# FFN input projection with the weights stationary and 256 tokens streamed, its product made feature-major and its transposes left out

## The reference

```python
D_MODEL, SEQ, D_FF = 2048, 256, 5632

def rmsnorm(x, g):
    y = x * lax.rsqrt(jnp.mean(x * x, axis=-1, keepdims=True) + EPS)
    return y * g

def swiglu(h, w_in, w_out):          # w_in 2048 x 11264, w_out 5632 x 2048
    gu = h @ w_in
    gate, up = gu[..., :D_FF], gu[..., D_FF:]
    return (jax.nn.silu(gate) * up) @ w_out

h = h + 0.5 * swiglu(rmsnorm(h, ffn1_norm[l]), ffn1_w_in[l], ffn1_w_out[l])
...
h = h + 0.5 * swiglu(rmsnorm(h, ffn2_norm[l]), ffn2_w_in[l], ffn2_w_out[l])
```

## Time and profile before

| | us |
|---|---|
| median of 3 runs | 2803.59 |
| the runs | 2803.33, 2803.59, 2807.78 |
| profiled execution: its own time | 2807.78 |
| profiled execution: span, first to last instruction | 2805.2 |
| TensorE (matmul) busy in the span | 2759.7 |
| weight loads busy | 2265.7 |
| VectorE busy | 1489.3 |
| ScalarE busy | 1272.2 |
| DMA | 506 MB, 180 GB/s |

### The profile page before, as it was taken

The page is one execution under the profiler, slowest core; times in us unless marked ns, Lnnn a source line. Parts: engine busy times, 40 slices in busy tenths (PEclk is TensorE's granted clock), DMA queues, the critical chain, the costliest instruction groups (busy, mean ns, idle before and its releaser), DMA issues.

```text
span 2805.2 us, 34347 instructions
## 1 busy us (share of the span) xinstructions
PE 2759.7 (98%) x12534; PEld 2265.7 (81%) x12534; DVE 1489.3 (53%) x1689; ACT 1272.2 (45%) x1621; POOL 57.1 (2%) x68
## 2 busy tenths in 40 slices
PE   8999999999999999999999999999999999999999
PEld 6888888888878788888888888877888778778877
DVE  5445455554634455555455455557655665555564
ACT  5443444344544445443444344544544444554443
POOL 0000000000000000000000000020000000120000
PEclk9999999999999999999999999999999999999999
DMA  8666666665645456655665665644456556546654
GB/s 276 189 188 194 189 190 190 193 190 162 205 137 165 149 193 187 191 188 192 190 188 191 192 193 162 201 158 150 150 186 187 159 185 188 156 139 195 181 154 139
DMA packets 375319, 506.04 MB, mean 180 GB/s; under 512 B 35831, under 2 KB 228545, under 8 KB 374417
## 3 DMA queue, kind: packets, MB, share of 16 engines
q1 hardware_dynamic: 373376, 495.84, 56.9%
q0 software_dynamic: 1632, 8.34, 0.8%
q10 hardware_dynamic: 176, 0.07, 0.0%
HBM read 502.03 MB, written 2.10 MB: 180 GB/s over the span
## 4 chain that ended last, share of the span: by engine, by line
PE 95%; DVE 2%; ACT 1%; POOL 1%; DMA 1%; issue 0%; SPq 0%; ACTq 0%; DVEq 0%
PE bank L1268 30%; PE bank L1270 29%; PE bank L1269 29%; PE bank L1226 2%; DVE wlo L1494 1%; ACT whi L1332 1%; DMA h<-in_x_dram 1%; POOL rope_b L849 1%; PE bank L996 0%; PE bank L797 0%; PE bank L781 0%; PE bank L1013 0%; PE bank L1022 0%; PE bank L488 0%; DVE iwork L922 0%
## 5 line engine op out<-in xcount | busy, mean ns | idle before, releaser
L1494 DVE TENSOR_TENSOR wlo<-raw,whi 128x1024 fp32r<-128x1024 f32 (+2 forms) x976 | 1154.7, 1187 | 1248.9 <-ACT whi L1332 1244.8
L1332 ACT CAST whi<-raw 128x1024 fp32r<-128x1024 f32 (+2 forms) x976 | 988.4, 1016 | 1374.9 <-PE bank L1270 1369.9
L1268 PE MATMUL bank<-whi,p_hi 128*128 128x512 f32 x2016 | 799.4, 397 | 5.9 <-DVE wlo L1494 5.8
L1270 PE MATMUL bank<-whi,p_lo 128*128 128x512 f32 x2016 | 787.1, 390 | 0.0
L1269 PE MATMUL bank<-wlo,p_hi 128*128 128x512 f32 x2016 | 786.6, 390 | 0.0
L1268 PE MATMUL bank<-whi,q_hi 128*128 128x512 f32 x1696 | 668.9, 394 | 5.3 <-DVE wlo L1494 5.2
L1270 PE MATMUL bank<-whi,q_lo 128*128 128x512 f32 x1696 | 661.5, 390 | 0.0
L1269 PE MATMUL bank<-wlo,q_hi 128*128 128x512 f32 x1696 | 661.2, 390 | 0.0
L1268 PEld LDWEIGHTS bank<-whi,p_hi 128*128 128x128 f32 x2016 | 379.9, 188 | 91.7 <-issue 15.3
L1269 PEld LDWEIGHTS bank<-wlo,p_hi 128*128 128x128 f32 x2016 | 380.1, 189 | 79.9 <-issue 3.1
L1270 PEld LDWEIGHTS bank<-whi,p_lo 128*128 128x128 f32 x2016 | 379.5, 188 | 80.5
(11 more groups left out here) (253 smaller groups left out, 954.7 us busy)
## 6 DMA issues: line engine op xcount, KB each, us to landing
raw<-in_ffn_w_in_dram SPq DMA_DIRECT2D x704, 256.0 KB, 2.9
raw<-in_ffn_w_out_dram SPq DMA_DIRECT2D x320, 256.0 KB, 3.0
raw<-in_w_in_a_dram SPq DMA_DIRECT2D x192, 256.0 KB, 3.0
raw<-in_w_in_mix_dram SPq DMA_DIRECT2D x128, 256.0 KB, 3.1
raw<-in_w_ple_gate_dram SPq DMA_DIRECT2D x128, 256.0 KB, 3.5
raw<-in_w_in_b_dram SPq DMA_DIRECT2D x128, 256.0 KB, 3.1
raw<-in_w_out_mix_dram SPq DMA_DIRECT2D x64, 256.0 KB, 3.2
raw<-in_w_o_a_dram SPq DMA_DIRECT2D x64, 256.0 KB, 3.4
```

The lines of the kernel that those rows point to most:

```text
L1268: pe.matmul(o, xht, wh, start=(kt == t_first), stop=False)
L1270: ins = pe.matmul(o, xlt, wh, start=False, stop=(kt == t_last))
L1332: act.copy(whi[:, c % SPLIT, 0:n, 0:w], raw[:, c, 0:n, 0:w]).then_inc(hi_done, 1)
L1494: dve.tensor_tensor(wlo[:, c % SPLIT, 0:n, 0:w], raw[:, c, 0:n, 0:w], whi[:, c % SPLIT, 0:n, 0:w].bitcast(F32), ALU.subtract).then_inc(lo_ ...
```

## The change

- In `ffn_in` stages `multiply` makes the weights stationary (128 features by 128 columns, four such blocks `m` of a tile's 512) and streams the 256 tokens. The gate sums of a round land in the first bank of its pair, the up sums in the second, both feature-major: 128 columns of the FFN on the partitions, tokens along the free axis.
- `rstd` is then needed along the free axis. `rstd_row` copies it into a 128x128 block for each half of the tokens (`rspread`), TensorE transposes the two blocks (L1105 of the changed kernel, behind chunk 1 of round 1 of `ffn1_in0` and `ffn2_in0`), VectorE copies the result to `rrow`, 256 tokens wide and the same on each partition.
- `evacuate` of `ffn_in` is now: VectorE multiplies the gate bank by `rrow` into `sg` and the up bank by `rrow` into `hid`, ScalarE applies silu to `sg` in SBUF, VectorE multiplies `hid` by `sg`. VectorE so waits for ScalarE in the middle.
- The transposes of `hid` are gone with their semaphore counts; ScalarE and VectorE split `hid` straight from SBUF (`hidden_hi`, `hidden_lo`) at the place where they split the bank before. `ffn_out` waits on `hid_done` in its first round.

The diff, cut to its core:

```diff
@@ -163,8 +163,9 @@
         h = sb("h", [P, TT, D])
-        at = overlaid([("tm", [P, TT, D], F32)], [("hid", [P, 2, TT, HB], F32)])
-        tm, hid = at["tm"], at["hid"]
+        at = overlaid([("tm", [P, TT, D], F32)],
+                      [("hid", [P, 2, 2, SEQ], F32), ("rspread", [P, TT, P], F32), ("rrow", [P, SEQ], F32)])
+        tm, hid, rspread, rrow = at["tm"], at["hid"], at["rspread"], at["rrow"]
         ab = overlaid([("bc", [P, 2, D], F32)],
@@ -287,10 +287,12 @@
-        n, latest = 0, {}
+        n, hids, latest = 0, 0, {}
         for s in stages:
                 b.number, latest[b.pair, b.kt], n = n, n, n + 1
+            if s.kind == "ffn_in":
+                s.hid0, hids = hids, hids + s.n
             for k in range(s.n):
@@ -1097,6 +1097,13 @@
                 filled(pe.transpose(use("gains")[:, 0:GAINS], vrow[0:GAINS, :], ident[0:GAINS, 0:GAINS]), "gains")
+            if stage in ROW_OF and (k, c) == (1, 1):
+                name = ROW_OF[stage]
+                pe.wait_ge(sem("rstd_spread"), int(name[-1]) + 1)
+                b = use(name)
+                for t in range(TT):
+                    ins = pe.transpose(b[:, t * P:(t + 1) * P], rspread[:, t, :], ident)
+                filled(ins, name)
             gla_pe(pe, stage, k, c)
@@ -1117,6 +1124,8 @@
             attention_b_dve(dve, link, stage, k, c)
+
+        ROW_OF = dict(ffn1_in0="rrow0", ffn2_in0="rrow1")
@@ -1203,26 +1212,16 @@
             def transposes(s, b, u):
-                number, parity, pair, kt, gain = resolve(s, b, u)
+                number, parity, pair, kt, gain = b.number, b.number % 2, b.pair, b.kt, b.gain
                 dst = bank[4 + parity]
-                if isinstance(b, Batch):
-                    issued[0] = number + 1
-                if not isinstance(b, Batch) or number >= 2:
+                issued[0] = number + 1
+                if number >= 2:
                     pe.wait_ge(freed_s[4 + parity], emitted[4 + parity])
-                if isinstance(b, tuple):
-
-                    pe.wait_ge(acc_free, s.a0 + b[1] + FREE0)
-                    src = [hid[:, (u - 1) % 2, t, j * P:(j + 1) * P] for j in range(2) for t in range(TT)]
-                elif isinstance(b.source, tuple):
-                    pe.wait_ge(acc_free, s.a0 + FREE0)
-                    src = [hid[:, b.source[0], t, j * P:(j + 1) * P] for j in range(2) for t in range(TT)]
-                else:
-                    src = b.source(kt)
-                for n, piece in enumerate(src):
+                for n, piece in enumerate(b.source(kt)):
                     ins = pe.transpose(dst[:, n * P:(n + 1) * P], piece, ident)
@@ -1252,6 +1251,16 @@
                 for j, kt in enumerate(tiles):
+                    if s.kind == "ffn_in":
+
+                        wh, wl = whi[:, c % SPLIT, j, :], wlo[:, c % SPLIT, j, :]
+                        for m in range(4):
+                            o = dst[m // 2][:, m % 2 * SEQ:(m % 2 + 1) * SEQ]
+                            f = slice(m * P, (m + 1) * P)
+                            pe.matmul(o, wh[:, f], xh[:, kt, :], start=(kt == t_first and m % 2 == 0), stop=False, skip_group_check=True)
+                            pe.matmul(o, wl[:, f], xh[:, kt, :], start=False, stop=False, skip_group_check=True)
+                            ins = pe.matmul(o, wh[:, f], xl[:, kt, :], start=False, stop=(kt == t_last), skip_group_check=True)
+                        continue
                     for t in range(TT):
@@ -1308,7 +1317,10 @@
                                 pe.wait_ge(sem("pool_split"), c + 1)
-                            pe.wait_ge(t_done, s.need[c])
+                            if s.kind == "ffn_out":
+                                pe.wait_ge(hid_done, s.hid_of.hid0 + s.chunk_tiles(c)[-1] // 2 + 1)
+                            else:
+                                pe.wait_ge(t_done, s.need[c])
                         ins = multiply(s, k, u, c, dst, tiles[0], 1 if s.kind == "ple" else tiles[-1])
@@ -1344,6 +1356,11 @@
+            def hidden_hi(s, k, u):
+
+                act.wait_ge(hid_ready, s.hid0 + k + 1)
+                act.copy(pair_hi[s.hid_pair][:, bass.ds(k * 2, 2), :], hid[:, u, :, :]).then_inc(hid_hi, 1)
+
             squared = [0]
@@ -1368,10 +1385,8 @@
                 if s.kind == "ffn_in":
-                    sums_done(act, s, k)
-                    for t in range(TT):
-                        ins = act.activation(sg[:, u, t, :], pair[t][:, 0:HB], ACT.Silu, scale=rstd[:, t:t + 1])
-                    ins.then_inc(silu_done, 1)
+                    act.wait_ge(scaled, s.hid0 + k + 1)
+                    act.activation(sgw[:, u, :], sgw[:, u, :], ACT.Silu).then_inc(silu_done, 1)
                 elif s.name in ("ffn1_out2", "mix_out", "ffn2_out2"):
@@ -1454,6 +1469,9 @@
                         operand_hi(s, b, u)
+                    made = hidden_of(s, k, u, peeled)
+                    if made:
+                        hidden_hi(*made)
@@ -1508,6 +1526,22 @@
+            def hidden_lo(s, k, u):
+
+                dve.wait_ge(hid_hi, s.hid0 + k + 1)
+                at_ = bass.ds(k * 2, 2)
+                dve.tensor_tensor(pair_lo[s.hid_pair][:, at_, :], hid[:, u, :, :], pair_hi[s.hid_pair][:, at_, :].bitcast(F32),
+                                  ALU.subtract).then_inc(hid_done, 1)
+
+            def rstd_row(name):
+
+                for t in range(TT):
+                    ins = dve.tensor_copy(rspread[:, t, :], rstd[:, t:t + 1].to_broadcast([P, P]))
+                ins.then_inc(sem("rstd_spread"), 1)
+                b = take(dve, name)
+                release(dve.tensor_copy(rrow[:, :], b[:, 0:SEQ]), name)
+                wait_freed(dve, name)
+
             def rms(n):
@@ -1521,11 +1555,13 @@
+                    sums_done(dve, s, k)
+                    row = rrow[:, :].unsqueeze(1).to_broadcast([P, 2, SEQ])
+                    dve.tensor_tensor(sg[:, u, :, :], pair[0][:, :].rearrange("p (j n) -> p j n", j=2), row, ALU.mult).then_inc(scaled, 1)
+                    dve.tensor_tensor(hid[:, u, :, :], pair[1][:, :].rearrange("p (j n) -> p j n", j=2), row, ALU.mult).then_inc(acc_free, 1)
+                    dve.wait_ge(acc_free, at_ + FREE0)
                     dve.wait_ge(silu_done, silu_before(s) + k + 1)
-                    for t in range(TT):
-                        ins = dve.scalar_tensor_tensor(hid[:, u, t, :], pair[t][:, HB:NB], rstd[:, t:t + 1],
-                                                       sg[:, u, t, :], ALU.mult, ALU.mult)
-                    ins.then_inc(acc_free, 1)
+                    dve.tensor_tensor(hid[:, u, :, :], hid[:, u, :, :], sg[:, u, :, :], ALU.mult).then_inc(hid_ready, 1)
                 elif s.kind in ("ffn_out", "mix_out", "ln_out"):
@@ -1629,12 +1665,17 @@
                         operand_lo(s, b, u)
+                    made = hidden_of(s, k, u, peeled)
+                    if made:
+                        hidden_lo(*made)
                     if not (peeled and k == s.n - 1):
                         rms(NORMED.index(s.name))
+                        if s.name in ROW_OF:
+                            rstd_row(ROW_OF[s.name])
                     evacuate(s, k, u)
                         angles(dve, link)
```

31 lines of the change are left out of this document (14 added, 17 removed).

## The result

| | us |
|---|---|
| median of the changed kernel (4 runs) | 2842.15 |
| its runs | 2840.90 to 2843.06 |
| median of the kernel before beside it (4 runs) | 2804.93 |
| ratio, 95% interval | 1.0128 [1.0116, 1.0140] |
| span of the profiled execution after | 2840.9 |

The changed kernel is 37.2 us slower. I had forecast 18.1 us faster and a range up to 2815: the sign was missed, and the time lies outside the range.

The account below looks back on a forecast made before the run. TensorE's rate of starting matmuls was taken as the bound. Transposes -20.2, split 0, row transposes +0.4 and stalls +1.7 gave -18.1 us, from 2803.6 to 2785.5 us; range 2781 to 2815, the forecast's own 2781 to 2791.

Parts of the forecast that it names:

- The step of 256 columns: ffn_in on TensorE: 4224 matmuls of 512 columns become 8448 of 256, step 0.1134 us, cost 0.
- Rival 2: TensorE matmuls: each instruction has a fixed part of 0.0031 us, +13.1 us, 2798.6 us in all; chance 0.12.
- Rival 1: ffn_in matmuls: successive loads hold back starts, step 0.1167 us, +27.9, 2813.4 us; chance 0.23, including steps up to 0.118.
- Rival 3: ffn_in weight loads not hidden behind 256 columns: +630 us, 3415 us; chance 0.04, shared with a far undersized wait.
- Transposes gone: TensorE in ffn_in: 176 transposes of hid removed, four in each of 44 rounds at 0.46 us a round, -20.2 us.
- row transposes: TensorE: two transposes of rspread in each of two stages, 4 x 0.11 us, +0.4 us.
- hand-over in `ffn1_in0`: After round 0 the evacuation chain starts late, so TensorE stalls before chunk 4 of round 1: +1.6 us, once.
- in `ffn2_in0`: The same late chain, without angles, before chunk 4: +0.1 us.
- Cost 0 in steady rounds and at `ffn1_out2`: Added ScalarE and VectorE work stays covered: 4.7 us slack in steady rounds, 0.5 us before chunk 6 of ffn1_out2.
- The signs that I named: Profile checks: step 0.113 us, two ffn_in rounds 43.5 us, one ffn1_in0 gap of 1 to 2 us; wrong above 0.1155.

Follow-up runs that it names:

- e1_half_stream: The kernel before, with each ffn_in matmul of 512 streamed columns issued as two of 256 on the same stationary block; 2859.04 us, ratio 1.0185.
- e7_long_streams: e4_old_product with stationary width and streamed length (288 to 512) set per ffn_in stage, inner tiles only, sums incomplete; 2643.37 us in one run.
- e3_stream_by_stage: The changed kernel with 248 down to 64 tokens streamed per ffn_in stage behind 128 stationary columns, sums incomplete; 2895.42 us in one run.
- e4_old_product: The changed kernel with the token-major product of 512 columns put back in ffn_in, output not the reference's; 2789.50 us, ratio 0.9937.

## Why the prediction failed

- **The step of 256 columns: this is what failed.** I wrote "By this row the split costs 0" and took 0.1134, half of 0.2268, with "no fixed part for an instruction". The step is 0.1200. That is above both ends of what I had bounded (0.1134 and 0.1167), and in place of 0 stands +55.8 us. Two errors lie in it. The one: I read the equality of the earlier trace rows with half of the earlier trace rows as proportionality. The earlier trace rows alone spoke against it: 512 columns at 2.4 GHz are 0.2133, and the step was 0.2268. With 13.3 ns in each 512-column step, half of it holds 6.7 ns of fixed part; that an 80-column block lands on the same number says nothing of proportionality, and why it does isn't known. The other: I treated the two narrow rows as the ends of a range for 128 columns, although I had noted that they were in no order by width; rows that I couldn't explain were no bound for a shape outside of them.
- **Rival 2 had the mechanism and not the size.** A fixed part for each matmul is what the runs show; the rival took 3.1 ns from the earlier trace rows and came to 2798.6; in float32r with a full block it is 13.3 ns. `e1_half_stream` shows it on the kernel before by itself, and `e7_long_streams` shows it at three more lengths. The Trainium skill, "TensorE: Matmul & The Clock Gate", Part 1, states about 2.5 ns for a warm matmul. In this case plain float32 comes near it with 3.1 ns, and float32r, with 13.3, doesn't. I had used to set the rival aside, and its chance of 0.12 was too low for a cost that one precision did show.
- **Rival 1** had the right sign, with a step lengthened by the loads to 0.1167. Its size was half of what came (0.0033 against 0.0066 us), and its ground (loads that follow one another hold back the start) isn't shown: `e1_half_stream` has the same step with one stationary operand for two halves. The load records number as many as the matmuls there too (16758 of each), so a cost of each load, and not of each stream, isn't excluded. Its 0.0033 us is eight ticks at 2.4 GHz, not the four that I wrote.
- **Rival 3, loads not hidden.** Right to set aside: with 128 to 224 streamed the step is 0.1117 (`e3_stream_by_stage`), just as in the earlier trace rows. By themselves were weak evidence: from the earlier trace rows a plain float32 stream of 128 columns takes by estimate 0.2157 - (0.4283 - 0.2157)/2 = 0.109 us, so that row needn't show a load at all.
- **Transposes gone, -20.2; row transposes, +0.4; hand-over in `ffn1_in0`, +1.6; in `ffn2_in0`, +0.1.** All stand as a sum. With `e4_old_product` these together are -16.8 measured for -18.1 worked out; in the changed kernel the stall was 1.48 us, and the second hand-over shows no gap.
- **Cost 0 in steady rounds and at `ffn1_out2`.** Stands: from 62 to 760 us no group of TensorE in the changed kernel has idle time, as before.
- **The sum with the measured step:** -20.2 + 0.4 + 1.6 + 55.8 = +37.6 us, measured +37.2.
- **The signs that I named** worked: the step was listed as the first thing to look at, with 0.1155 as the point above which the forecast is wrong.

What stays open: what makes up the 13.3 ns (the load of each matmul or its stream), and why narrow blocks have less at 256 streamed columns, the same at 384 and more at 512. Orientation and the PSUM region are excluded; a change of the input's precision alone wasn't tried.

## What to carry to other kernels

Where TensorE starts one matmul behind the other without idle time, count instructions as well as streamed columns: here, in float32r with full blocks and 256 to 512 columns streamed, a step was the columns at 2.4 GHz plus 12 to 16 ns, so cutting 512 into 2 x 256 costs 6%, more than removing four transposes from a hundred matmuls gives (2%). Measure the very shape that a change will issue before relying on a neighbour's; a narrow block's step said nothing of a full one here. And when a product's layout is wrong for the next one, look first at idle engines for the re-ordering: here VectorE and ScalarE did it in some 2.6 us each a round without making TensorE wait in a steady round; the first hand-over was the place to watch.

## What the runs showed of the hardware that I had not expected

- The part of 13.3 ns in a float32r step that doesn't grow with the stream (full blocks; 256, 320, 384 and 512 columns), four times the 3.1 ns of plain float32.
- The step as a function of the stationary width jumps: 0.1133 at 112, 0.1162 at 96, 0.1135 at 80, 0.1172 at 48 in one kernel; 112 at 0.1179 in another with the other orientation.
- Shorter streams can be slower. 64 columns behind loads of 128 took 0.2133 a step at a granted clock of 0.50, against 0.1117 for 128 columns at 1.00, in a TensorE that the records show as never idle.
- A wait of 2.16 us cost some 1.6 us more than itself: the clock was down behind it until 60.6 us. The wait of 1.32 us in the changed kernel was followed by a single slower start (0.22 us).
- Streams of 512 (in two pieces) and 256 in turns cost 6.6 ns a pair more than each in its own sequence, and 512 columns behind a run of 288 took 0.2309 a step for 0.2267.
- VectorE transposes 128x512 in 32x32 blocks in 0.71 us, and a 32x128 copy to other partitions is 0.23 us on VectorE and 0.31 us on ScalarE; TensorE's way to the same layout was 0.46 us of the engine that had no time.
